# Turning an older tile's normalised output in the first attention stage of a hybrid decoder step

## The reference, cut to what matters

```python
s = jnp.einsum('bqhcd,bkhcd->bchqk', qf, kf) * (HEAD_DIM ** -0.5)
s = jnp.where(mask, s + bias, -jnp.inf)
p = jax.nn.softmax(s, axis=-1)
w = p[:, 0] - lam * p[:, 1]
o = jnp.einsum('bhqk,bkhe->bqhe', w, v.astype(jnp.float32))
o = o * lax.rsqrt(jnp.mean(o * o, axis=-1, keepdims=True) + SUBLN_EPS)
o = o * subln_g.astype(jnp.float32) * (1.0 - lam_init)
```

## Time and profile before

| | |
|---|---|
| three runs, us | 1539.07, 1541.85, 1542.25 (median 1541.85) |
| the profiled execution, us | 1539.33, its span 1537.5 |
| PE busy | 1331.1 us (87% of the span) |
| PE weight loads | 959.6 us (62%) |
| DVE busy | 794.5 us (52%) |
| ACT busy | 663.0 us (43%) |
| POOL busy | 146.7 us (10%) |
| mean granted PE clock | 0.941 of full speed |

### The profile page before, as it was taken

How to read it: one execution, slowest core, us unless ns; L and a number is a source line. 1 busy time by engine, 2 the same in 40 slices (tenths; PEclk the granted TensorE clock), 3 DMA queues, 4 the chain that set the end, 5 groups by cost and what they waited for, 6 DMA issues and landing times. The chain is left out here.

```text
span 1537.5 us, 26150 instructions
## 1 busy us (share of the span) xinstructions
PE 1331.1 (87%) x8895; PEld 959.6 (62%) x8895; DVE 794.5 (52%) x1078; ACT 663.0 (43%) x1078; POOL 146.7 (10%) x175
## 2 busy tenths in 40 slices
PE   7999999997798979768999898699739999999940
PEld 6877888885565656445656564588626666667620
DVE  4321122103556555637777777644455666666637
ACT  5410222013556556545556565422225555555512
POOL 1000000000000000000000000000011222222026
PEclk9999999998999989989999999899859999999975
DMA  5622332176687868547789794354357997632277
GB/s 198 199 93 72 125 114 93 57 236 192 215 285 236 302 211 295 193 163 241 250 263 314 246 327 162 118 165 151 143 224 256 409 413 273 226 115 105 82 281 258
DMA packets 159644, 319.14 MB, mean 208 GB/s; under 512 B 21815, under 2 KB 50906, under 8 KB 155418
## 3 DMA queue, kind: packets, MB, share of 16 engines
q1 hardware_dynamic: 146666, 274.48, 52.2%
q0 software_dynamic: 7200, 26.22, 5.0%
q10 hardware_dynamic: 5648, 16.78, 2.7%
HBM read 318.79 MB, written 55.77 MB: 244 GB/s over the span
## 5 line engine op out<-in xcount | busy, mean ns | idle before, releaser
L2372 DVE TENSOR_TENSOR w_gate_up_split<-w_gate_up,w_gate_up_split 128x2048 fp32r<-128x2048 f32 x64 | 143.8, 2288 | 117.3 <-ACT w_gate_up_split L2421 117.3
L2326 PE MATMUL gate_up_ps<-w_gate_up_split,slot_rows_T 128*128 128x512 f32 x768 | 185.8, 398 | 13.4 <-DVE slot_rows_T L2380 13.4
L325 PE MATMUL proj_ps<-w_in_split,x_T_hi 128*128 128x512 f32 x576 | 186.4, 399 | 0.0
L2326 PEld LDWEIGHTS gate_up_ps<-w_gate_up_split,slot_rows_T 128*128 128x128 f32 x768 | 143.3, 190 | 47.0 <-DVE slot_rows_T L2380 18.0
L1176 PE MATMUL turns_and_scores_ps<-ident,pages 128*128 128x128 f32 (+1 forms) x1088 | 147.6, 281 | 17.5 <-DVE sample_rest_products L1435 5.3
L1176 PEld LDWEIGHTS turns_and_scores_ps<-ident,pages 128*128 128x128 f32 (+1 forms) x1088 | 122.8, 146 | 53.5 <-issue 52.9
L2421 ACT ACTIVATE w_gate_up_split<-w_gate_up 128x2048 fp32r x64 | 119.1, 1908 | 47.4 <-issue 33.6
L325 PEld LDWEIGHTS proj_ps<-w_in_split,x_T_hi 128*128 128x128 f32 x576 | 109.2, 190 | 26.0
L459 ACT ACTIVATE proj_rows<-proj_ps,sum_squares 128x512 f32<-128x512 f32 x36 | 24.8, 688 | 230.6 <-PE proj_ps L325 230.6
L2348 PE MATMUL expert_out_ps<-w_down,expert_act_T 128*128 x256 | 115.3, 593 | 1.3 <-ACT expert_out L2451 1.3
L325 PE MATMUL proj_ps<-w_in_split,x_T_lo 128*128 128x512 f32 x288 | 115.1, 400 | 0.0
(11 more groups left out here) (228 smaller groups left out, 1928.6 us busy)
## 6 DMA issues: line engine op xcount, KB each, us to landing
pages<-in_cache_s SPq DMA_DIRECT2D x256, 256.0 KB, 4.3
pages<-in_cache_d SPq DMA_DIRECT2D x226, 256.0 KB, 4.4
w_gate_up<-in_w_gate SPq DMA_DIRECT2D x34, 1024.0 KB, 8.2
w_gate_up<-in_w_up SPq DMA_DIRECT2D x34, 1024.0 KB, 10.1
w_down<-in_w_down SPq DMA_DIRECT2D x34, 1024.0 KB, 12.2
scratch_moe_out<-expert_out ACTq DMA_DIRECT2D x32, 512.0 KB, 3.9
w_in_now<-in_w_in SPq DMA_DIRECT2D x48, 256.0 KB, 2.9
pages_ahead<-in_cache_d SPq DMA_DIRECT2D x30, 256.0 KB, 3.5
```

What stands on the lines that cost most here:

```text
L325: last = pe.matmul(pj_ps[:, n % PJ_BANKS, :], h[:, k, at], w[g % 2][:, k, :], start=(k == 0 and m == 0), stop=(k == KC - 1 and m == 2))
L2326: last = pe.matmul(gu_ps[:, u, :], xT[:, u, a, k, :], gu_split[:, u, b, k, :], start=(k == 0 and m == 0), stop=(k == KC - 1 and m == 2))
L2372: dve.tensor_tensor(gu_split[:, u, 1, at, :].rearrange("p k (c n) -> p k c n", c=2), raw[:, at, :, :], gu_split[:, u, 0, at, :].bitcast(F3 ...
```

## The change

In DIFF the step `turn_out` between a tile's turns and its product takes the output of two tiles ago in place of the last one. The second tile's place has none, and the two last ones stand together at the end of the stage. No engine's code for a step is changed.

```diff
@@ -748,7 +748,7 @@
             out += soft(*one, 1) if one else []
             out += scores(*two) if two else []
             out += turns(it, i)
-            out += [(("turn_out", *tiles[n - 1]), 3)] if n else []
+            out += [(("turn_out", *tiles[n - 2]), 3)] if n >= 2 else []
         else:
             out += turns(it, i)
             out += soft(*one, 1) if one else []
@@ -758,7 +758,7 @@
         if i == 1 and it:
             out.append((("store", it - 1), 0))
     if kind == DIFF:
-        out.append((("turn_out", *tiles[-1]), 3))
+        out += [(("turn_out", *tile), 3) for tile in tiles[-2:]]
     return out + [(("store", TURNS - 1), 0)]
```

## The result

The changed kernel takes 1549.53 us (median of 7 runs, 1543.40 to 1557.38), the kernel before 1539.63 in 7 runs: a ratio of 1.0066, 95% interval 1.005 to 1.0082. So it is slower, by some 10 us, where the forecast was 1543.5 and next to no difference (+1.7). The time is that of rival 3 (1549.5), and it lies 0.03 us above the range's upper end; but both were counted from the median of three runs, 1541.85, and the difference of rival 3 was +7.6, not 9.9.

What follows compares the result with a forecast made beforehand. PE was taken to set the DIFF stage; terms 0.2 - 1.5 - 1.4 - 1.3 + 2.7 + 0 + 1.4 + 1.2 = +1.3 us, raised to +1.7, gave a 1543.5 us median, range 1537.5 to 1549.5.

Steps and rivals of the forecast that it cites:

- rival 3: Slower: sample exponential behind the product in tile 1.2, plus low clock and lost covers; +7.6 us, 1549.5, chance 0.34.
- The reading of the queue: PE's 28.1 us wait at L1165 comes from L1321's turn in the DVE's queue, not POOL; direct effect +0.2 us.
- Rival 1: PE's waits at L1165 do go, up to 28.1 us less, 1513.8 to about 1530; chance 0.04.
- The stage's end: Transposition of tile 30's output now stands before the last one, mostly within a 0.75 us wait; 0 to 0.4, taken +0.2.
- tile 0.1: No `turn_out` there any more, so PE's 1.51 us wait behind a DVE page copy goes; taken -1.5 us.
- tile 1.0: Maxima of tile 1.1 now precede the copy of page 13, so PE's 1.73 us wait mostly goes; taken -1.4.
- tile 2.2: Maxima of tile 2.3 go before the long sample maximum; PE's 7.3 us wait loses 1.3.
- L1165 in tile 1.1: Page 15's copy falls directly before L1321 and page 16 behind `turn_out`; bounds 0 and +2, taken +1.4 us.
- The exponential of tile 1.2: ACT's 2.01 us sample exponential falls behind the product, to the head of tile 1.3, delaying PE's sample transpositions; +2.7 us.
- the clock term: Further idle time near tile 1.2 may hold PE at the 1.2 GHz level longer; bounds 0 and +3, taken 0.
- A few smaller ones of both signs: Remaining swaps, tiles 0.3, 1.3, 1.5 up and 2.1, 3.0, 3.2 down; together 0.
- half of the lost covers: Steps now behind `turn_out` no longer cover its wait; four places without PE slack, +2.4 at most, half taken, +1.2.

Runs made afterwards that it cites:

- e1: Kernel before with the older output turned, but the missing step's three units kept, so all 200 sample steps stand as before; 1541.24 us, ratio 1.0002.
- e4: Older output and old sample order, with the DVE's normalisation (L1321) moved ahead of the next tile's maxima; 1535.99 us, ratio 0.9959 to the kernel before.
- e7: Kernel before, still turning the last tile's output, with its normalisation moved to the head of the tile; 1568.97 us, ratio 1.018.
- e2: Kernel before, still turning the last output, with the sample steps where the changed kernel has them; 1551.51 us, ratio 1.0068.
- e14: Kernel before with the older output and only the 19 moved sample steps of turn 1; 1545.03 us, ratio 1.004.
- e17: Kernel before with the older output and the 38 moved sample steps of turns 1 and 2 together; 1549.18 us, ratio 1.0058.
- e3: Changed kernel with turn 1's sample exponential put back ahead of the product of tile 1.2; 1544.82 us, ratio 1.0023 to the kernel before.
- e8: Changed kernel with ten unused PE transpositions added between product 1.2 and the sample transpositions; 1544.79 us, ratio 1.0021 to the kernel before.
- e9: Changed kernel with page 6 of turn 2 put back before the exponentials of tile 1.6; 1544.19 us, ratio 1.0038 to the kernel before.
- e10: Changed kernel with both turn 1's sample exponential and page 6 of turn 2 put back; 1545.79 us, ratio 1.0034 to the kernel before.
- e5: Kernel before with only turn 1's sample exponential moved behind the product of tile 1.2; 1541.68 us, ratio 1.001.
- e11: Kernel before with only page 6 of turn 2 moved behind the exponentials of tile 1.6; 1538.69 us, ratio 0.999.
- e13: Kernel before with the older output and only the 13 moved sample steps of turn 0; 1537.25 us, ratio 0.998.
- e15: Kernel before with the older output and only the 19 moved sample steps of turn 2; 1540.85 us, ratio 1.0006.
- e16: Kernel before with the older output and only the 9 moved sample steps of turn 3; 1538.62 us, ratio 1.0002.

## Why the prediction was wrong, by its own steps

**Right.** The reading of the queue: "L1321 is itself a queued DVE instruction, and the question is what it is late for". Rival 1 is refuted by e1 and by the 32.1 us that the PE still waits, and e4 and e7 show both halves of the reason. The Trainium skill's page Perfetto Trace Analysis (Optimization Strategy) has one find the semaphore behind the gap and make that dependency start sooner. Rows and rule agree only if the dependency is followed one step further, to the instruction's own queue: e1 had the awaited input earlier and gained nothing, within 2.3 us; e4 moved the place and gained 5. The stage's end cost 0.26 us for the 0.2 taken. By the PE's idle time, after less before, the gains came: tile 0.1 -1.5 (-1.5 taken; e1 has 1.0 of it, so that much belongs to the missing step), tile 1.0 -1.7 (-1.4), tile 2.2 -2.8 (-1.3; but against e1, which has the old order, only -0.5). L1165 in tile 1.1 waited 1.56 us in place of 0.15 (+1.4 taken). The exponential of tile 1.2 made the PE wait 2.88 us in place of 0.18 (+2.7 taken), of which tiles 1.2 and 1.3 together show 1.6. So most of the single waits that had a term were sized well, and the sum still missed by some 8 us.

**Wrong: "Bounds 0 and +3; I take 0"**, the clock term. This is the first step that failed. It was looked at in tile 1.2 only, while the added wait in tile 1.1, which I had priced at +1.4 for its length, comes first. After, around the end of that wait:

```profile
470.92 0.33 PE L1165 MATMUL turns_and_scores_ps<-ident,o_normed 128*128 128x128 f32 x1 [1.56 <-DVE o_normed L1321]
```

```profile
468.00:472.00 4.00, 2.44 (x27) 1.65 (x26) 2.66 (x6) 1.27 (x5) 0.00 (x0) 1.00 0.98 317
472.00:480.00 8.00, 7.59 (x55) 4.62 (x54) 3.93 (x11) 3.85 (x11) 0.74 (x2) 0.57 1.06 374
484.00:492.00 8.00, 5.22 (x18) 3.21 (x19) 2.05 (x3) 6.37 (x11) 0.74 (x2) 0.50 0.00 0
```

and before, in the same place:

```profile
468.00:472.00 4.00, 3.85 (x43) 1.93 (x39) 2.98 (x7) 2.26 (x8) 0.00 (x0) 1.00 0.99 268
472.00:476.00 4.00, 3.25 (x39) 2.19 (x35) 2.41 (x8) 2.26 (x7) 0.76 (x2) 1.00 0.98 343
```

Before, the PE was busy 3.85 of 4 us there and kept its full level until tile 1.2. After, it was busy 2.44 of 4, and of the 8 us behind that, 7.59 of them in work, it ran some 6.9 at the low level (by the mean of 0.57); the second low stretch follows in its place, and lasts longer. A fall behind that wait is seen in e2 too (0.57 in 472 to 476) and in e14 (0.50 in 468 to 476), not in e17 (1.00). In all, the clock fell within 2 us behind that transposition in seven of the eight profiled executions with this order in tile 1.1 (after, e2, e3, e8, e9, e10, e14, not e17), and in none of the seven that have tile 1.1 as before (before, e1, e5, e11, e13, e15, e16), where the wait is 0.15 us. The stretch table gives the price beside e17: 0.8 us in e2, 3.7 in e14, 5.1 in after; over the whole stage the PE is busy 10.2 us longer in after than before, and 4.2 in e2, with the same instructions. e8 shows that idle time in tile 1.2 is part of it. e1 is busy 4.6 us longer than before in the old order and is not slower in its median, so one execution does not size this term; its place is shown, and its size only as some 1 to 10 us. The Trainium skill's page TensorE: Matmul & The Clock Gate (What's actually happening) lets an idle array fall to the low level; I had cited it for the upper bound of this very term and took the lower one. The trace agrees that the low level comes behind idle time of the PE, here already behind a wait of 1.56 us.

**Wrong: "A few smaller ones of both signs (tiles 0.3, 1.3, 1.5 up, ...), together 0."** The second step that failed. In idle time of the PE tile 1.5 cost 1.6 us in place of 0, and tiles 0.6 and 2.3, for which I had no term, cost 1.0 to 1.4 and 1.1: some 3.8 us together, in e2 as in after, and for tile 1.5 in e14 and e17 too. Tile 0.3 cost at most 0.5. Each of these swaps seemed cheap since it moved one instruction by one place; what I did not do for them is ask which ring place or which copy stands behind it.

**Wrong: half of the lost covers, "I take half, +1.2".** The four steps that I named stand in tiles 0.2 (page 16), 1.7, 2.4 and 2.5 (the applies), and the PE's idle time there grew by 0.7, 0.6, 0.5 and 0.6 us: 2.3 us, close to the bound of 2.4. In the tiles right behind them (0.3, 2.0, 2.6) it did not fall, so nothing was given back there.

**Wrong: the addition.** Price by price the list sums places as if they were independent. e3, e8, e9 and e10 show that they are not: a wait removed here can shift the low stretches and the slack of the next tile.

Rival 3 named the mechanism with its place and the low clock, and gave 1549.5, 0.03 us from the median; that closeness is luck in part: it took the order's gains at about a third of what this execution shows (-2.1 for -6.0), left out tiles 0.6, 1.5 and 2.3, and started from a median 2.2 us too high, and these errors cancel. What remains open: why the clock does not fall in e17, and why the four turns add to +2.8 per mille and the whole to +6.6. Low stretches that an earlier turn's order moves into a later one would do it, and after has a further one at 516 to 520 us (0.63) that before, e2 and e14 do not have. That is argued, not shown.

## What to carry to other kernels

A wait names the instruction that ended it, and that instruction may be late for its own turn in its own queue: look at what the releasing engine did just before, and whether it ever idled for the input that you are about to make earlier. If it did not, the older input is worth nothing until the instruction is moved up (here 33 us between doing one and doing both). Where a plan is driven by counted units, keep the units of a step that you remove, or the edit reorders what comes behind it; and price such a reordering by running it alone, since small swaps here neither cancelled nor added. To see where it costs, split each stretch with the same work into idle and busy time of the bounding engine: here idle time told what the order did, and busy time that grew with the same instructions told what the clock did.

## What the runs showed of the hardware that I had not expected

Idle time of the PE has a price beyond its length. Ten transpositions that nothing needs, in a gap of 2.9 us, made the kernel 7 us faster (e8 against after). The same eight transpositions took 1.97 us at the low level and 1.09 at the full one. A clock fall came behind a wait of 1.56 us among work, in seven of eight executions. In one stretch with the same steps, six executions took 64.2 to 73.3 us, and their order by time is that of their granted clock within each of the two orders of steps. Over whole runs it is alike: in the changed kernel the run of 1543.40 us had a mean clock of 0.938, the one of 1557.38 had 0.931. So one profiled execution of this kernel tells a term of a few us only to within that scatter, and a place is believed here only where several executions agree. A slower PE is not always a loss: in tile 2.2, where the PE waits for a chain of the DVE and ACT, it waited 7.3 us before and 5.0 in e1, whose PE had come there later.
